# Exchanging the rotary halves of queries and keys by transfers within SBUF instead of matmuls with a sign matrix

## What is computed

```python
def apply_rope(x, cos, sin):
    half = x.shape[-1] // 2
    x1, x2 = x[..., :half], x[..., half:]
    cs = cos[:, None, :].astype(x.dtype)
    sn = sin[:, None, :].astype(x.dtype)
    return jnp.concatenate([x1 * cs - x2 * sn, x2 * cs + x1 * sn], axis=-1)
```

## Time and profile before

| | |
|---|---|
| median of three runs | 4062.28 us (4060.51 to 4065.91) |
| span of the profiled execution | 4060.6 us, 0.1 us above the fastest of the runs |
| TensorE matmuls | 3735.7 us busy, 92% |
| VectorE | 2144.5 us busy, 53% |
| ScalarE | 1404.4 us busy, 35% |
| DMA | 273.29 MB, mean 67 GB/s |
| second block, layer 0 | about 1100 to 2740 us |
| second block, layer 1 | about 2790 to 4010 us |

### The profile page before, as it was taken

The page is one execution under the profiler, slowest core; times in us unless marked ns, Lnnn a source line. Parts: engine busy times, 40 slices in busy tenths (PEclk is TensorE's granted clock), DMA queues, the critical chain, the costliest instruction groups (busy, mean ns, idle before and its releaser), DMA issues.

```text
span 4060.6 us, 55626 instructions
## 1 busy us (share of the span) xinstructions
PE 3735.7 (92%) x20595; PEld 2873.8 (71%) x20595; DVE 2144.5 (53%) x3596; ACT 1404.4 (35%) x2502; POOL 0.2 (0%) x4
## 2 busy tenths in 40 slices
PE   5988989999799999999798999988999999798998
PEld 3655778878667787777586676876668777585666
DVE  3555345553555525777623555245563677636654
ACT  2433233332233313444412444122332444424432
POOL 0000000000000000000000000000000000000000
PEclk8988999999899999999899999998999999899999
DMA  7444235542101121111021111211113111131122
GB/s 250 138 113 102 85 96 156 163 151 91 37 26 28 29 63 42 41 36 41 16 67 42 27 32 32 68 57 35 34 30 88 47 49 49 32 82 37 37 63 78
DMA packets 491969, 273.29 MB, mean 67 GB/s; under 512 B 40170, under 2 KB 477510, under 8 KB 491823
## 3 DMA queue, kind: packets, MB, share of 16 engines
q1 hardware_dynamic: 470770, 249.98, 21.8%
q10 hardware_dynamic: 21052, 21.33, 1.7%
HBM read 269.05 MB, written 10.32 MB: 69 GB/s over the span
## 4 chain that ended last, share of the span: by engine, by line
PE 80%; DVE 10%; ACT 3%; issue 2%; DVEq 2%; DMA 1%; ACTq 0%; SPq 0%
PE ps L556 75%; PE ps L972 3%; PE ps L921 2%; DVE w_low L552 1%; ACT w_high L542 1%; DVE neg_max L836 1%; DVE probs L1380 1%; DVEq L1261 1%; ACT probs L804 1%; DMA w_raw<-in_w_in 0%; DVE probs L825 0%; DVE y_low L2397 0%; DVE probs L1842 0%; DVE y_and_merged L1389 0%; DVE probsT L1029 0%
## 5 line engine op out<-in xcount | busy, mean ns | idle before, releaser
L556 PE MATMUL ps<-h_high,w_high 128*128 128x512 f32 (+1 forms) x3432 | 1285.1, 374 | 68.9 <-DVEq L2601 22.1
L556 PE MATMUL ps<-h_low,w_high 128*128 128x512 f32 (+1 forms) x3432 | 1249.0, 364 | 0.0
L556 PE MATMUL ps<-h_high,w_low 128*128 128x512 f32 (+1 forms) x3432 | 1245.6, 363 | 0.0
L556 PEld LDWEIGHTS ps<-h_high,w_high 128*128 128x128 f32 x3432 | 652.8, 190 | 234.7 <-issue 87.0
L552 DVE TENSOR_TENSOR w_low<-w_raw,w_high 128x1024 fp32r<-128x1024 f32 x374 | 448.6, 1200 | 635.6 <-ACT w_high L542 612.5
L556 PEld LDWEIGHTS ps<-h_high,w_low 128*128 128x128 f32 x3432 | 654.0, 191 | 104.1
L556 PEld LDWEIGHTS ps<-h_low,w_high 128*128 128x128 f32 x3432 | 654.9, 191 | 92.9 <-issue 2.2
L542 ACT ACTIVATE w_high<-w_raw 128x1024 fp32r<-128x1024 f32 x374 | 387.6, 1038 | 610.6 <-PE ps L556 490.8
L804 ACT ACTIVATE probs<-ps,neg_max 128x768 f32<-128x768 f32 (+1 forms) x240 | 194.6, 814 | 441.2 <-DVE neg_max L836 441.1
L556 PE MATMUL ps<-probsT,v 128*128 128x512 f32 (+4 forms) x736 | 286.5, 559 | 10.3 <-DVE probsT L1029 8.8
L836 DVE TENSOR_REDUCE neg_max<-ps 128x1 f32<-128x768 f32 (+1 forms) x240 | 196.7, 847 | 177.9 <-PE ps L556 166.7
(11 more groups left out here) (229 smaller groups left out, 4017.0 us busy)
## 6 DMA issues: line engine op xcount, KB each, us to landing
w_raw<-in_w_in SPq DMA_DIRECT2D x436, 256.0 KB, 3.1
y_and_merged<-in_w_mod SPq DMA_DIRECT2D x96, 256.0 KB, 3.1
w_raw<-in_w_branch SPq DMA_DIRECT2D x96, 256.0 KB, 3.0
w_raw<-in_w_up SPq DMA_DIRECT2D x88, 256.0 KB, 4.3
y_and_merged<-in_w_ada SPq DMA_DIRECT2D x64, 256.0 KB, 3.3
w_raw<-in_w_out SPq DMA_DIRECT2D x48, 256.0 KB, 3.1
w_raw<-in_w_down SPq DMA_DIRECT2D x44, 256.0 KB, 3.0
y_and_merged<-in_w_ada SPq DMA_DIRECT2D x4, 2048.0 KB, 20.1
```

The source lines that it names most:

```text
L556: return nc.tensor.matmul(*a, **kw)
```

## The change

In the three units stages the exchange of the two halves is done by DMAs issued by SyncE, from the query (or key) in SBUF to another place in SBUF. The sign goes into the sine table; the two matrices become plain permutations and are still used in `pre` and `swapre`.

- `swap_halves` issues 4 DMAs of 32 partitions x 2 KB (64 KB each) for 64-feature heads, and 2 DMAs of 16 partitions x 2 KB (32 KB each) for `mla`. `diff` does it for Q and then for K.
- `sp_swap` waits for the copy of Q (`mla`) or of Q and K (`rope_in`). In `mla` it stands behind the loads of the unit after it, in `diff` and `swa` behind the loads of the same unit's body.
- `dve_rope_swapped` waits for the transfers. In `mla` it works on the 32 rotary partitions instead of 96.
- `pe_rope` goes. `v_steps` of `mla` waits for `q_out` instead of `roped`, `qk_steps` of `swa` for `rope_in` instead of `roped`, and `pe_proj_z` of `diff` gets a wait for `rope_in`.
- In `swa` the rotary step on VectorE stands behind chunk 2 instead of 1, the rounding on ScalarE behind chunk 4 instead of 3, the remainders on VectorE behind chunk 5 instead of 4.

```diff
-    c["sin_hd"] = np.tile(np.sin(ah), (4, 1)).astype(np.float32)
+    c["sin_hd"] = np.tile(np.concatenate([-np.sin(ah), np.sin(ah)]), (2, 1)).astype(np.float32)
...
-            r[b + m + 32, b + m] = -1.0
+            r[b + m + 32, b + m] = 1.0
...
+        QS = PP[:, 4608:5120]
+        QS2 = YM[:, 14 * TOK:14 * TOK + LAT]
+        KS2 = YM[:, 14 * TOK + LAT:14 * TOK + 2 * LAT]
...
+        def swap_halves(sp, dst, src, first, n, key):
+
+            for a in range(first, 128 if n == 32 else 96, 2 * n):
+                sp.dma_start(dst[a:a + n], src[a + n:a + 2 * n, 0:LAT]).then_inc(S[key], 16)
+                sp.dma_start(dst[a + n:a + 2 * n], src[a:a + n, 0:LAT]).then_inc(S[key], 16)
+
+        def sp_swap(sp, s, t, per, off):
+
+            if s["name"] == "mla":
+
+                sp.wait_ge(S["q_out"], cnt(s, "q_out", t, per, off + 1))
+                swap_halves(sp, QS, Q, 64, 16, "swap_q")
+                return
+
+            sp.wait_ge(S["rope_in"], cnt(s, "rope_in", t, per, off + 1))
+            if s["name"] == "diff":
+                swap_halves(sp, QS2, Q, 0, 32, "swap_q")
+                swap_halves(sp, KS2, KB[:, 0, :], 0, 32, "swap_k")
+            else:
+                swap_halves(sp, QS, Q, 0, 32, "swap_q")
...
                         load_split(sp, s, t, 2, u, cols(win2[l], i * 128 + C_Z))
-                    repeat(sp, 8, 2, body)
+                        if not (isinstance(i, int) and i == 0):
+                            sp_swap(sp, s, t, 2, u - 1)
...
                         for j, c in enumerate((C_DQ, C_DK, C_DV, C_Z + 1024)):
                             load_split(sp, s, t, 4, j, cols(win2[l], i * 128 + c))
+                        sp_swap(sp, s, t, 1, 0)
...
                         load_split(sp, s, t, 2, 2, cols(win2[l], i * 128 + (C_SQ + 128)))
+                        sp_swap(sp, s, t, 1, 0)
...
-                pe.wait_ge(S["roped"], cnt(s, "roped", t, ui, u))
+                pe.wait_ge(S["rope_in"], cnt(s, "rope_in", t, ui, u))
...
-        def pe_rope(pe, s, t, u, name):
...
             if name == "mla":
-                pe.wait_ge(S["roped"], cnt(s, "roped", t, ui, u + 1))
+
+                pe.wait_ge(S["q_out"], cnt(s, "q_out", t, ui, u + 1))
...
             elif name == "diff":
+
+                pe.wait_ge(S["rope_in"], cnt(s, "rope_in", t, ui, u + 1))
                 pe_split(pe, s, t, 4, 3, 128, tgroups(2, s["cq"]))
...
+        def dve_rope_swapped(dve, s, key, each, t, per, off, x, swapped, cos, sin):
+
+            dve.wait_ge(S[key], t * (each * per) + (s.base[key] + each * (off + 1)))
+            v = nc.vector
+            v.tensor_tensor(x, x, cos, ALU.mult)
+            v.tensor_tensor(swapped, swapped, sin, ALU.mult)
+            v.drain()
+            v.tensor_tensor(x, x, swapped, ALU.add).then_inc(S["roped"], 1)
+            v.drain()
...
-                    evac_twin(act, s, t, u, i, 0, lambda c: act_qk_high(act, nxt, t, u, i + 1) if c == 3 else None)
+                    evac_twin(act, s, t, u, i, 0, lambda c: act_qk_high(act, nxt, t, u, i + 1) if c == 4 else None)
...
-                    if c == 1:
+                    if c == (2 if name == "swa" else 1):
                         dve_proj_qk(dve, nxt, t, u, i + 1)
...
-                    if c == (4 if name == "swa" else 5) and not s["first"]:
+                    if c == 5 and not s["first"]:
                         dve_qk_low(dve, nxt, t, u, i + 1)
```

More of the change, by code:

```diff
@@ L85, in shape_constants @@
     for m in range(16):
[L86 removed]
+        r[64 + m + 16, 64 + m] = 1.0
         r[64 + m, 64 + m + 16] = 1.0
@@ L146, in add @@
             now[k] = now.get(k, 0) + v
-    keys = ("h n square added square_mm rstd scaled high low_row lat_sq lat_ss lat_rs lat_ri lat_sp lat_n rinv spread fin down_ev x_t mm_ev rope_in rope_mm roped q_mm k_mm k_out q_out kv_ev kv_low vt_in vt_mm v_ev z_ev tanh scores maxed exped normed "
+    keys = ("h n square added square_mm rstd scaled high low_row lat_sq lat_ss lat_rs lat_ri lat_sp lat_n rinv spread fin down_ev x_t mm_ev rope_in rope_mm roped q_mm k_mm k_out q_out kv_ev kv_low vt_in vt_mm v_ev z_ev tanh swap_q swap_k scores maxed exped normed "
             "pt_act pt_dve rl_mm transposed o_done o_sq o_ss o_rs y bias merged up_ev gelu f_high f_low y_low y_high y_round m_high m_low out_ev ctx_in mod_copy mod_sum qk_high qk_low").split()
@@ L175, in plan @@
             if s["name"] == "mla":
-                add(s, q_mm=n, q_out=n, kv_ev=n, kv_low=n, v_ev=n, z_ev=n, tanh=n, rope_mm=n, roped=n)
+                add(s, q_mm=n, q_out=n, kv_ev=n, kv_low=n, v_ev=n, z_ev=n, tanh=n, swap_q=32 * n, roped=n)
             if s["name"] == "diff":
-                add(s, vt_in=n, vt_mm=n, v_ev=n, z_ev=n, tanh=n, rope_mm=2 * n, roped=2 * n, q_out=n, o_sq=n, o_ss=n, o_rs=n)
+                add(s, vt_in=n, vt_mm=n, v_ev=n, z_ev=n, tanh=n, swap_q=64 * n, swap_k=64 * n, roped=2 * n, q_out=n, o_sq=n, o_ss=n, o_rs=n)
             if s["name"] == "swa":
-                add(s, z_ev=n, tanh=n, rope_mm=n, roped=n)
+                add(s, z_ev=n, tanh=n, swap_q=64 * n, roped=n)
         elif k == "merge":
@@ L471, in body @@
                         load_split(sp, s, t, 2, u, cols(win2[l], i * 128 + C_Z))
-                    repeat(sp, 8, 2, body)
+                        if not (isinstance(i, int) and i == 0):
+                            sp_swap(sp, s, t, 2, u - 1)
+                    body(0, 0, 0)
+                    body(0, 1, 1)
+                    with sp.Fori(1, 4) as t:
+                        for u in range(2):
+                            body(t, u, t * 2 + u)
+                    sp_swap(sp, s, 3, 2, 1)
                 elif name == "diff":
@@ L1429, in moved @@
             for key, per in (("h", s["nh"]), ("n", s["nn"]), ("v_ev", 1), ("vt_in", 1), ("vt_mm", 1), ("z_ev", 1), ("q_out", 1), ("q_mm", 1), ("rope_in", 1), ("tanh", 1), ("kv_ev", 1), ("kv_low", 1),
-                             ("qk_high", 1), ("qk_low", 1), ("roped", 2 if s["name"] == "diff" else 1), ("rope_mm", 2 if s["name"] == "diff" else 1), ("y", s["subs"])):
+                             ("qk_high", 1), ("qk_low", 1), ("roped", 2 if s["name"] == "diff" else 1), ("swap_q", 32 if s["name"] == "mla" else 64), ("swap_k", 64), ("y", s["subs"])):
                 m.base[key] += per
@@ L1449, in prologue @@
                     pass
-                pe_rope(pe, s, 0, 0, name)
                 for _ in v_steps(pe, s, 0, 0, 0):
@@ L1516, in step @@
                     pe_scores(pe, s, t, u, i, 0, swa_side(t, u, i), nz + n_side)
-                    pe_twin_values(pe, s, t, u, i, lambda: pe_rope(pe, nxt, t, u, name), free=lambda: z_taken(t, u))
+                    pe_twin_values(pe, s, t, u, i, free=lambda: z_taken(t, u))
                     return
@@ L1520, in step @@
                     pe_scores(pe, s, t, u, i, 0, qkv_steps(t, u, i), n_side)
-                    pe_values(pe, s, t, u, i, 0, lambda: pe_rope(pe, nxt, t, u, name))
+                    pe_values(pe, s, t, u, i, 0)
                     pe_turn_v(pe, nxt, t, u)
@@ L1538, in step @@
                 else:
-                    pe_values(pe, s, t, u, i, 0, lambda: pe_rope(pe, nxt, t, u, name), values, 3)
+                    pe_values(pe, s, t, u, i, 0, side=values, n_side=3)
                 for _ in values:
```

11 lines of the change are left out of this document (6 added, 5 removed).

## The result

| | before | after |
|---|---|---|
| median | 4064.1 us (4060.5 to 4069.7) | 4086.2 us (4085.0 to 4088.2) |
| span of the profiled execution | 4060.6 us | 4084.6 us |

The ratio is 1.0055, with a 95% interval of 1.0043 to 1.0067: slower by 22 us, where 4058.0 and a range up to 4081 had been forecast. No step of the work became much slower; nearly every part moved by a few microseconds. So the two traces are compared stage by stage: a prologue runs from the first copy of Q to the first scores, a step from one unit's first scores to the next unit's.

The account below looks back on a forecast made before the run. It took TensorE as 80% of the chain, but VectorE as ending last in the steps' values, shading most of 55 us of matmuls. Terms -2.8 - 0.7 - 4.2 - 4.0 + 3.0 + 4.4 = -4.3 us gave 4058.0, range 4045 to 4081.

Parts of the forecast that it names:

- step (b): Price of a swap: spacing of issues on SyncE's queue, 0.3 to 0.5 us, taken as 0.4.
- (a): Price of a swap: SyncE's wake-up, estimated at 0.2 us from 0.17 us between a release and the released instruction.
- (c): Price of a swap: issue to landing of 64 KB, taken as 2.0 us between bounds 1.9 and 2.5.
- Rival 1: Late swap, slower: `swa` steps lose beyond swaps of 3.7 us (layer 0) or 4.0 (layer 1); 4083, chance 0.23.
- `swa` steps: 14 steps: chunk 3's product starts earlier, -0.2 us a step in layer 0, -0.4 in layer 1; -4.2 us.
- `diff` prologues: Two prologues: K's halves land late, so TensorE waits for the gate's weights; +3.0 us (+1 to +5.5).
- `mla`: 14 steps -0.7 us; two prologues -4.0 us, v block starting earlier, part given back by a lower clock.
- `diff` steps: 14 steps: swaps land in time, VectorE's wait for the matmul goes, -0.2 us each; -2.8 us.
- `swa` prologues: Two prologues: the rotary step waits for the swap with nothing beside it, +2.2 us each; +4.4 us.
- Rival 3: The clock falls, slower: TensorE idles up to 2.0 us in `diff` steps, costing 37 us; 4095, chance 0.07.
- Rival 2: The matmuls count, faster: `swa` steps gain 12.6 us instead of 4.2, with swaps of 3 us or less; 4049.6, chance 0.20.
- the far case of 4014: Matmul time would count in `diff` and `mla` steps too, the 55 us coming off; 4014, chance 0.03.

Follow-up runs that it names:

- `swa` alone: The swap in the `swa` stage only, with `mla` and `diff` keeping their rotary matmuls as in the kernel before: 4075.6 us, 1.0033.
- diff_steps: Against the swap in `diff` alone, the first unit of `diff` has its matmuls back, so only units 1 to 7 swap: 4063.2 us, 0.9992.
- pool_both: The changed kernel with GpSimd issuing the second head's transfers in `swa` and four of the eight in `diff`, beside SyncE: 4072.1 us, 1.0017.
- keep_each: The changed kernel with the 64 rotary matmuls kept, results unused; in `diff` Q's rotary step waits for Q's own matmul alone: 4089.4 us, 1.0055.
- chunks_as_before: The changed kernel with `swa`'s rotary step, rounding and remainders put back one chunk earlier, as in the kernel before: 4110.9 us, 1.0119.

## Why the prediction was wrong

**The price of a swap: step (b) failed, (a) and (c) held.** Wake-up 0.03 us (0.2 taken), landing 2.0 (2.0 taken), but 0.56 to 0.64 us from issue to issue, where 0.4 was taken from between two readings of one row group and 0.5 was the upper bound. The reading was wrong already: a merged row of two issues lasts one interval plus the second issue, not two intervals. The 1.00 us of the two weight loads are these two, 0.63 us apart:

```profile
1203.94 0.37 SPq L367 DMA_DIRECT2D w_raw<-in_w_in  x1
1204.57 0.37 SPq L367 DMA_DIRECT2D w_raw<-in_w_in  x1
```

In the kernel before, the weight loads of `w_in` issued one behind the other (228 pairs) start 0.56 us apart in the median, so the price stood in its trace. (The 0.17 us that (a) was taken from are an idle time of VectorE and not a wake-up; the estimate was high, at no cost.) Four transfers took 3.85 us and not 3.4, eight took 6.4 and not 5.0, above the upper bound of 6.2. With chunk 3's copy done 0.8 us after the rotary step (0.5 taken) and the rotary step 2.06 (2.2 taken), the product of a layer-0 step comes 0.6 us later than worked out: from -0.3 to +0.3 us a step, which is what the step measured. Rival 1 had put the break-even at 3.7 us in layer 0, and was right about the mechanism; its chance of 0.23 was too low. In layer 1 it put the break-even at 4.0 us, and there the steps lost 0.05 to 0.57 us with swaps of 3.9: this size was off.

**`swa` steps**, -4.2 predicted, +8.0 in the trace: 6 of it the two jumps, which no step of the prediction had. They are a landing of 3.3 us beside an instruction fetch plus a fall of the clock. The other 6 us of the difference are the late swap, some 0.5 us in each of the other steps. (The first step of layer 0 is 1.0 us shorter than before, with `swa` alone too; no run shows why.)

**`diff` prologues**, +3.0 predicted, +10.7 in the trace: the failed term is K's landing, 5.0 us behind the copy, measured 7.6 in layer 0: seven intervals of 0.63 instead of 0.4, and a last landing of 3.2 beside a fetch. TensorE idled 6.98 us where 3.4 (1556.3 to 1559.7) was worked out: the gate's matmuls came 2.5 us later still, and TensorE was there 1.1 us earlier, since with the rotary matmuls a wait of 0.96 us for K's copy went too. Of the kernel before:

```profile
1547.86 1.13 PE L556 MATMUL ps<-qT,rot_hd 128*128 128x512 f32 x2 [0.96 <-ACT y_and_merged L1213]
```

And I had not asked there what I had asked of the `mla` prologue: what the clock does behind the gap; the term stood at nothing. It fell, and the first 4.84 us of matmuls ran at half speed, some 2.4 us more. 1.7 + 2.6 + 2.4 = 6.7, against 6.6 measured in layer 0. In layer 1 the swap took 6.4 us, TensorE idled 5.29 and the low clock lasted 3.4 us, for +4.1 us. That both belong to the prologues is shown by `diff_steps`, that the series is a cause by `pool_both`; that the low clock costs 2.4 us is worked out, no run took it away alone.

**`mla`**: -4.0 predicted for the prologues, -2.7 in the trace. But the give-back by the clock, which the prediction put there, falls in the first step behind each (+1.4 and +2.5). Prologue and first step together are -1.7 us in layer 0, near the -2.0 predicted, and +2.9 in layer 1 (+0.5 to +3.1 in nine other kernels with this swap), where no gain was left. The rest of the steps' +6.2 (for -0.7) is swaps that landed late beside fetches, after 2.8 us in layer 0 and 3.4 and 3.0 in layer 1, and 0.1 us a step for which I have no cause. The measured ratio of the stage, 1.0003 (0.9994 to 1.0012), leaves out the -4.7 us (0.9988) of the prediction: the term failed too, with +1 us measured.

**`diff` steps and `swa` prologues** came as predicted (-3.6 for -2.8, +5.4 for +4.4). In the `diff` steps that was luck in part: K's halves landed 1.4 us later than taken and were still in time, by about 1 us. Most signs listed for the profile after came too; of the signs against, three struck: issues more than 0.5 us apart everywhere, seven of 224 transfers that landed after more than 2.5 us, and VectorE waiting for them (0.45 to 0.80 us) in three `mla` steps. Rival 3 as put, a fall inside the `diff` steps, did not come at idle pieces of 1.43 us; it came in `swa` at 2.05 us and behind the prologue at 6.98. Rival 2 asked for swaps of 3 us or less, and was right in that: with two queues they took 3.0, and `swa`'s steps gained 0.4 to 0.7 us each, until the clock and a late issue took it back. In the changed kernel no swap of four transfers was that short.

The low end of the sum was mis-added: the bounds one way come to -3.5 - 1 - 10 - 6.4 + 1 + 3.4 = -16.5 us, not -19. The measured time lies on the other side.

The matmuls in the shade were judged right at first order, and the far case of 4014 never stood open; but `keep_each` shows 0.3 to 0.5 us for two of them in a `diff` step, not nothing.

## What to carry to other kernels

Price a series of small transfers by the issue interval, from start to start and of the very form and queue (here 0.63 us on SyncE, 0.5 on GpSimd), once for each transfer but the last, plus one landing (2.0 us), and not by bytes. Read the interval from the rows of single issues, since a merged row holds one interval fewer than issues; where somebody waits for it, split the series over two queues or keep the matmul, and use the transfer only where its consumer comes later than that sum. Ask of every gap that a change opens on TensorE, the prologues' too, what the granted clock does behind it: a delay of 1.3 us cost 3. And leave a margin of over a microsecond for transfers on which a step waits, since single ones land late.

## What the runs showed of the hardware

- A transfer from SBUF to SBUF of 32 or 64 KB lands 1.9 to 2.0 us after its issue. Its issue occupies SyncE's queue for 0.51 us (the first) to 0.59, and the next starts 0.56 to 0.64 us after it. A weight load's issue of 256 KB took 0.37 us, and the next started 0.56 us after it in the median.
- Sometimes one issue of a series, the fourth or a later one, takes 1.3 to 1.9 us, always with a landing of 2.8 us or more in the same series (six series in these traces). Twice GpSimd's second issue started 2.0 us late. What they wait for isn't in the profile.
- Instruction fetches of 16 KB share the DMA engines with the kernel's transfers. In the `swa` stages they came every 20 us or so, and of the transfers in flight beside one, 20 in 68 landed after 2.9 us or more. Code size and the place of a loop can so move a step by 3 us.
- The granted clock fell to 0.50 behind idle pieces of 2.05 and 2.27 us of TensorE inside a `swa` step, and didn't behind 1.00 in `swa` or 1.43 us in `diff`. The length of the piece alone doesn't decide it: in `chunks_as_before` 14 pieces of 2.0 to 2.3 us brought 7 falls. And behind the 1.71 us piece with which steps 2 to 7 of `swa` begin in layer 0, in the kernel before as well, it fell in no step before and in up to four in other runs. The Trainium skill (TensorE: Matmul & The Clock Gate, Part 1) has it follow how busy the engine has recently been; the runs agree in that delaying TensorE's input brought more falls and keeping idle matmuls fewer.
